# The order of the last group of a feed-forward in two token halves: the first half's out products ahead of the second half's gate

## The reference

```python
def swiglu(h, w_in, w_out):
    g, u = jnp.split(h @ w_in, 2, axis=-1)
    return (jax.nn.silu(g) * u) @ w_out
...
x = x + gt_f * rmsnorm(swiglu(h, w_ffn_in[l], w_ffn_out[l]), g_post_ffn[l])
...
def sandwich(x, fn, g_pre, g_post, shift, scale, gate, res_w):
    h = modulate_2(rmsnorm_2(x, g_pre), shift, scale)
    y = rmsnorm_2(fn(h), g_post)
    return x + res_w * gate[:, None, :] * y
```

## Time and profile before

| | |
|---|---|
| time, median of 3 runs | 2835.96 us (2835.62 to 2836.16) |
| time of the profiled execution | 2833.18 us |
| its span, first to last instruction | 2831.4 us |
| mean granted TensorE clock | 0.987 of full speed |
| PE busy | 2736.9 us, 97% |
| DVE, POOL, ACT busy | 1595.9, 1230.3, 1078.3 us |

### The profile page before, as it was taken

One profiled execution on the slowest core, in us unless ns is written; L12 is line 12 of the kernel. 1 busy time (PEld: TensorE's weight loads), 2 busy tenths in 40 slices (PEclk: granted clock), 3 DMA queues, 4 the chain that ended last, 5 costly groups with the idle time before them and its releaser, 6 DMA issues.

```text
span 2831.4 us, 41285 instructions
## 1 busy us (share of the span) xinstructions
PE 2736.9 (97%) x15742; PEld 2360.6 (83%) x15742; DVE 1595.9 (56%) x2593; ACT 1078.3 (38%) x1817; POOL 1230.3 (43%) x643
## 2 busy tenths in 40 slices
PE   8989999999999999899999999999999999999998
PEld 6778788888899799888888888888877788888887
DVE  6788565667777668655565555655553522422223
ACT  3267333223444457442222332222454833422222
POOL 0333444445555533344455344554433344444443
PEclk7999999999999999999999999999999999999999
DMA  5323555434576312424444334443323233133321
GB/s 236 97 57 94 193 198 189 149 134 135 178 241 228 107 37 60 142 92 161 148 156 156 120 134 149 156 170 134 107 66 105 82 97 97 58 107 96 96 89 60
DMA packets 103865, 361.70 MB, mean 128 GB/s; under 512 B 12449, under 2 KB 14625, under 8 KB 102305
## 3 DMA queue, kind: packets, MB, share of 16 engines
q1 hardware_dynamic: 103714, 359.63, 38.5%
HBM read 338.61 MB, written 2.10 MB: 120 GB/s over the span
## 4 chain that ended last, share of the span: by engine, by line
PE 85%; DVE 8%; ACT 2%; DMA 2%; issue 2%; POOL 1%; SPq 0%; ACTq 0%; DVEq 0%
PE ps L346 71%; PE ps L2264 3%; PE ps L2252 2%; PE ps L2234 2%; PE ps L760 1%; PE ps L570 1%; DVE negm L2313 1%; PE ps L422 1%; DVE dump L405 1%; DMA raw<-w_stream 1%; PE ps L2457 1%; PE ps L2026 1%; PE ps L2237 1%; ACT w_hi L317 1%; DVE h_lo L619 1%
## 5 line engine op out<-in xcount | busy, mean ns | idle before, releaser
L323 POOL TENSOR_TENSOR w_lo<-raw,w_hi 128x1024 fp32r<-128x1024 f32 x421 | 1069.8, 2549 | 1226.4 <-ACT w_hi L317 1193.6
L317 ACT ACTIVATE w_hi<-raw 128x1024 fp32r<-128x1024 f32 x441 | 460.3, 1056 | 1167.0 <-PE ps L346 1098.8
L346 PE MATMUL ps<-n_hi,w_hi 128*128 128x512 f32 (+1 forms) x1744 | 640.0, 367 | 10.5 <-DVE n_lo L867 9.5
L346 PE MATMUL ps<-n_lo,w_hi 128*128 128x512 f32 (+1 forms) x1744 | 628.1, 360 | 0.0
L346 PE MATMUL ps<-n_hi,w_lo 128*128 128x512 f32 (+1 forms) x1744 | 628.0, 360 | 0.0
L346 PEld LDWEIGHTS ps<-n_hi,w_hi 128*128 128x128 f32 x1744 | 329.7, 189 | 66.3 <-DVE n_lo L867 9.8
L346 PE MATMUL ps<-h_hi,w_hi 128*128 128x512 f32 (+1 forms) x1096 | 364.7, 348 | 8.8 <-DVE h_lo L619 3.8
L346 PEld LDWEIGHTS ps<-n_lo,w_hi 128*128 128x128 f32 x1744 | 329.9, 189 | 51.1 <-issue 1.9
L346 PEld LDWEIGHTS ps<-n_hi,w_lo 128*128 128x128 f32 x1744 | 329.6, 189 | 49.6
L346 PE MATMUL ps<-h_lo,w_hi 128*128 128x512 f32 (+1 forms) x1096 | 357.4, 341 | 0.0
L346 PE MATMUL ps<-h_hi,w_lo 128*128 128x512 f32 (+1 forms) x1096 | 357.1, 341 | 0.0
(11 more groups left out here) (325 smaller groups left out, 3806.2 us busy)
## 6 DMA issues: line engine op xcount, KB each, us to landing
raw<-w_stream SPq DMA_DIRECT2D x441, 512.0 KB, 3.7
modraw<-mod_stream SPq DMA_DIRECT2D x128, 512.0 KB, 3.8
mod_extra<-mod_stream SPq DMA_DIRECT2D x48, 512.0 KB, 4.8
mod_pair<-mod_first SPq DMA_DIRECT2D x7, 1024.0 KB, 12.5
l_qs<-l_q_hi SPq DMA_DIRECT2D x32, 128.0 KB, 2.3
l_qs<-l_q_lo SPq DMA_DIRECT2D x32, 128.0 KB, 2.3
l_qs<-l_q_hi SPq DMA_DIRECT2D x16, 192.0 KB, 2.9
l_qs<-l_q_lo SPq DMA_DIRECT2D x16, 192.0 KB, 3.5
```

Of the source, the lines that this page charges most:

```text
L317: nc.scalar.activation(w_hi[:, c % RING, :], raw[:, c % RING, :], ACT.Copy).then_inc(hi_ready, 1)
L323: nc.gpsimd.tensor_tensor(w_lo[:, c % RING, :], raw[:, c % RING, :], w_hi[:, c % RING, :].bitcast(F32), ALU.subtract).then_inc(lo_ready, 1)
L346: mm = nc.tensor.matmul(out, w[a], x[b][:, off:off + n], start=first and i == 0, stop=last and i == 2)
```

## The change

In the last group of the three feed-forwards the order becomes: gate and up of the first half, all out products of the first half, gate of the second half with the four post sums of the first half inside it, up of the second half with the spread of the first half inside it, out products of the second half. The out products of a half are now written as all eight products on the first hidden block, then a wait for the low part, then all eight on the second; before, only the four even ones went ahead of that wait. Pre sums of the first half stand after products 1, 4 and 7 of the second pass (before: 4, 6 and 7). The second half's up moves from PSUM bank 1 to bank 3, since bank 1 is now in use by `post_two`. ACT does the first half's squares and root before the second half's silu, with a second `root_ahead` after that silu and the split of block c + 4 behind it. DVE does total and inverse before `mult(1)` and places the first two `post_two` around `low(1)`. POOL does the three `post_added` before the split of d0.

```diff
-    HALF_GATE, HALF_UP, HALF_OUT, PRODUCTS = (3, 0), (1, 1), ((5, 6, 2, 7), (5, 6, 0, 7)), 1
+    HALF_GATE, HALF_UP, HALF_OUT, PRODUCTS = (3, 0), (1, 3), ((5, 6, 2, 7), (5, 6, 0, 7)), 1
...
-        def outs(e, between, beside):
-            for n in range(0, KC, 2):
-                out(e, n, [0])
-                if n == 6 and between:
-                    between()
-            pe.wait_ge(half_hid_lo, 2 * j + e + 1)
-            for n in range(KC):
-                mm = out(e, n, [1] if n % 2 == 0 else [0, 1])
-                if e == 1 and n == KC - 1:
-                    mm.then_inc(w_used, 2)
-                elif n % 2 == 1:
-                    mm.then_inc(half_out, 1)
-                if n in beside:
-                    beside[n]()
+        def outs(e, beside):
+            off, w = HALVES[e]
+            for b in range(2):
+                if b == 1:
+                    pe.wait_ge(half_hid_lo, 2 * j + e + 1)
+                for n in range(KC):
+                    mm = product(tiles(c + 2 + b)[n], (f["hi"][:, b, :], f["lo"][:, b, :]),
+                                 [(half(HALF_OUT[e][n // 2], n % 2), off, w)], (b, n % 2) == (0, 0), (b, n % 2) == (1, 1))
+                    if b == 1 and e == 1 and n == KC - 1:
+                        mm.then_inc(w_used, 2)
+                    elif b == 1 and n % 2 == 1:
+                        mm.then_inc(half_out, 1)
+                    if b == 1 and n in beside:
+                        beside[n]()
...
         pe.wait_ge(hid_ready, CREDIT + f["m"] + 2 * g + 1)
-        part_block(1, 0, HALF_GATE[1])
         pe.wait_ge(lo_ready, c + 4)
         pe.wait_ge(out_free, CREDIT + 8 * g)
-        outs(0, None, {5: post(0, 0), 7: post(0, 1)})
-        part_block(1, 1, HALF_UP[1], {1: post(0, 2), 3: post(0, 3)})
+        outs(0, {})
+        part_block(1, 0, HALF_GATE[1], {2: post(0, 0), 4: post(0, 1), 6: post(0, 2), 7: post(0, 3)})
+        pe.wait_ge(half_silu, 2 * j + 1)
+        part_block(1, 1, HALF_UP[1], {5: lambda: post_spread(pe, h, 0)})
...
-            outs(1, lambda: post_spread(pe, h, 0), {})
+            outs(1, {})
...
-        outs(1, lambda: post_spread(pe, h, 0), {4: pre(0), 6: pre(1), 7: pre(2)})
+        outs(1, {1: pre(0), 4: pre(1), 7: pre(2)})
...
         hidden_hi(0)
+        root_ahead()
+        for i in range(HPAIRS):
+            post_square(act, h, 0, i)
+        post_root(act, h, 0)
         silu(1)
         root_ahead()
         split_hi(act, c + RING)
-        for i in range(HPAIRS):
-            post_square(act, h, 0, i)
         hidden_hi(1)
-        post_root(act, h, 0)
...
+        post_total(dve, h, 0)
+        post_inverse(dve, h, 0)
         mult(1)
-        post_total(dve, h, 0)
+        post_two(dve, h, 0, 0, post_slot, PRODUCTS)
         low(1)
-        post_inverse(dve, h, 0)
+        post_two(dve, h, 0, 1, post_slot, PRODUCTS)
...
-            split_lo(pool, d0)
             for j in range(ADDED):
                 post_added(pool, h, 0, j)
+            split_lo(pool, d0)
```

More of the change, by code:

```diff
@@ L1124, in part_block @@
                     after[k]()
-        def out(e, n, bs):
+        def outs(e, beside):
             off, w = HALVES[e]
[L1128 to L1131, removed]
-        def outs(e, between, beside):
-            for n in range(0, KC, 2):
-                out(e, n, [0])
-                if n == 6 and between:
-                    between()
-            pe.wait_ge(half_hid_lo, 2 * j + e + 1)
-            for n in range(KC):
-                mm = out(e, n, [1] if n % 2 == 0 else [0, 1])
-                if e == 1 and n == KC - 1:
-                    mm.then_inc(w_used, 2)
-                elif n % 2 == 1:
-                    mm.then_inc(half_out, 1)
-                if n in beside:
-                    beside[n]()
+            for b in range(2):
[10 more added lines that the diff above has]
+                        beside[n]()
         def post(e, i):
@@ L1406, in last_halves_dve @@
             add(0, i)
+        post_total(dve, h, 0)
+        post_inverse(dve, h, 0)
         mult(1)
-        post_total(dve, h, 0)
+        post_two(dve, h, 0, 0, post_slot, PRODUCTS)
         low(1)
-        post_inverse(dve, h, 0)
+        post_two(dve, h, 0, 1, post_slot, PRODUCTS)
         if h == 4:
-            post_two(dve, h, 0, 0, post_slot, PRODUCTS)
-            post_two(dve, h, 0, 1, post_slot, PRODUCTS)
             for i in range(HPAIRS):
@@ L1422, in last_halves_dve @@
             return
-        for i in range(HPAIRS):
-            post_two(dve, h, 0, i, post_slot, PRODUCTS)
+        post_two(dve, h, 0, 2, post_slot, PRODUCTS)
+        post_two(dve, h, 0, 3, post_slot, PRODUCTS)
         add(1, 0)
```

## The result

The changed kernel takes 2841.23 us (median of 13 executions; 2836.62 to 2845.88) against 2835.96 us (13 as well; 2832.43 to 2837.67): ratio 1.0017, with a 95% interval of 1.0009 to 1.0025. Run a second time, it came to 1.0010 (1.0001 to 1.0019). So it is slower by about 0.1 to 0.2%. That is inside the forecast's bound of "no change"; the median lies on the upper edge of the forecast's range (2841.2).

What follows compares the result with a forecast made beforehand. TensorE, busy 97% of the span, was taken as the bound, so order matters only where PE stands still. 2 x 0.3 (order) + 2 x 1.3 (clock) - 0.75 (end) = +2.45 us on 2835.96: 2838.4, range 2834.6 to 2841.2.

Steps and rivals of the forecast that it cites:

- POOL's and ACT's queues: In h = 1 and 2, ACT's late split and POOL's two splits delay the first pre sum; PE idles about 3.2 us.
- The out block: First half's out products wait for POOL's low parts of both out blocks: a new PE stall of 0.46 us.
- The order without the clock: Last groups of h = 1 and 2: +0.3 us each before the clock is counted, bounds 0 and +1.0.
- The clock: After the idle in h = 1 and 2, 3.4 us at half clock cost 1.3 us each, bounds 0 and 1.5.
- Rival A: Clock stays at 1.00 after the pause in one or both stages: 2835.8, or 2837.1 with one fall; chance 0.27.
- The end: In h = 4, DVE's residual products after the adds start 0.75 us earlier: -0.75 us, bounds -0.3 and -1.2.
- nothing changes: In h = 4, from the residual products after the adds to the end, DVE sets the pace and no time changes.
- upper bounds: Order at most +1.0 and clock 1.5 us in each of h = 1 and 2; h = 4 at -0.3 us.
- Rival B: POOL is done sooner, pre sums are not late, DVE products set the gain: -4.95 us, 2831.0; chance 0.05.
- rival C: POOL is later still, with longer idle and half clock; with 1 us more, +7.85 us, 2843.8; chance 0.07.

Runs made afterwards that it cites:

- best version: Changed kernel with ACT's c + 4 split before the root, POOL's pre pairs before c + 5's split, second out block awaited only at use: 0.9968, 0.9972 of kernel before.
- idle filled: Changed kernel plus seven unread matmuls ahead of the first pre sum in h = 1 and 2: 0.9988 and 0.9993 of the kernel before.
- early split: Changed kernel with ACT's split of block c + 4 ahead of the root: 0.9985 of the kernel before, median 2833.12 us against 2836.70.
- later load: Changed kernel with ACT's second root_ahead (table load and root) behind both splits instead of ahead of them: 0.9994 of the kernel before.
- first pair ahead of c + 5: Changed kernel with POOL's first pre pair between its splits of c + 4 and c + 5: 1.0010 of the kernel before.

## Why the prediction was right

**POOL's and ACT's queues.** Every step from the root to the first pre sum came where the prediction had it, counted from the group's start: ACT's split 20.89 us in (predicted 20.77), POOL's splits 22.01 (21.89), the first pre sum 27.46 (27.4). Its idle was 3.23 (3.2). The kernels that move ACT's split or the load show that this path is the cause, and the later load that time taken off it goes whole out of PE's idle (1.49 us of each).

**The out block.** 0.35 us of idle, predicted 0.46 from issue to issue (6.26 from the gate to the first out product, less 5.76, gives 0.50 on that scale). The row names no releaser, but POOL's splits of the out blocks end at 1590.85, 0.10 us before that product starts, and without the wait for the second of them, in the best version, the idle is gone. In h = 4 of the best version, where only this wait differs, the group is 0.57 us shorter than with the new order alone (40.14 to 40.71).

**The order without the clock.** Predicted +0.3 a group, measured +0.2 (idle filled).

**The clock.** Predicted to fall in both groups, at 1.3 us each; it fell in all four groups of the two traces, and costs 1.51. The prediction took off 0.2 us for a part of the 3.4 us that could lie in the idle itself. None did: the fall came 0.3 to 1.3 us after PE had gone on, so all 3.4 us were paid. Rival A (no fall in one or both groups) did not happen in these two traces; what the other executions did is not known.

The Trainium skill ("TensorE: Matmul & The Clock Gate", section on HAM oscillation) has the group after such a wait begin at the low clock. The traces agree that the clock falls, but the work after the wait began at 1.00 and kept it for 0.3 to 1.3 us.

The drain of 1380 ns that the Trainium skill ("ScalarE: Activation LUTs", section on what ACT_TABLE_LOAD costs) adds to every switch is not seen: in the chain above 0.01 us lies between each load and the operation behind it and 0.02 us ahead of the second load, and moving that load together with its root took away 1.49 us of idle, not 2.5 or more.

**The end.** Predicted -0.75 us. With the clock at 0.50 at the last spread the old order takes 41.96 us and the new one 41.21: -0.75. With the fall behind the spread the new order takes 40.71, and the old one, with the fall near the spread's end, 41.49: -0.78. So the term was right, like against like; but "nothing changes" from the residual products on left out the spread, which is PE's and costs half a microsecond more or less by the clock, in either order. In the traces of the new order it ran at the low clock in five of nine (in a sixth for part of it), in neither of the best version, and in one of two of the old order; whether the order makes that likelier stays open.

With 0.2 and 1.5 us in each of the two groups and -0.75 at the end the sum is +2.65, where +2.45 was forecast. The largest error of size is in the clock, 0.2 us a group, and half of that is made up by the order, 0.1 us a group the other way. By the two traces as they fell the groups give 3.1 and 3.2 us. The medians differ by 5.3 us and, the second time, by 3.6; the intervals reach from 2.6 to 7.1 and from 0.3 to 5.4 us, and no run here tells whether what is over 3.2 us is more than the spread of the executions. The longer stretch between the groups of h = 1 and 2, 2.9 and 2.6 us in the two traces, would cover it. That the first median still lies on the edge of the range is partly luck: the forecast's own upper bounds add up to +4.7 us, 2840.7, and the range reached 0.5 us further without a term for it.

Rival B (pre sums not late) and rival C (idle of over 4 us) did not happen in the changed kernel. The best version shows a time like B's to be there once both queues are put right: B was given -4.95, it has -5.9, of which 0.57 in h = 4 come from the out block's wait, which B did not move.

## What to carry to other kernels

When work moves on one engine, write down for every other engine what now stands in front of its next urgent item. Here PE's order gained, and the split of a block that PE did not need for another 16 us had slid behind a root and two table loads in ACT's queue, and with its neighbour in front of an urgent pair in POOL's. Look for the engine's idle time before its waits, and put the work that is not urgent there: that turned +0.1% into -0.3%. And a wait on PE has two prices, the wait and the matmuls after it; a filler of unread matmuls separates the two in one run.

## What the runs showed of the hardware that was not expected

With two waits of 0.94 and 1.24 us, 3 us apart, came 10.2 us at granted clock 0.50 in one group and 3.4 us in the next, while single waits of 1.41 to 1.44 us (kernel before, early split) left it at 1.00 and those of 1.74 us (later load) did not. Cutting this wait in two didn't save the clock, then.

But the length of a wait alone doesn't decide. Some 8 to 10 us ahead of the groups of h = 1 and 2, in code that no run changes, PE waits for `y` in every trace, and the wait differs from one execution to the next. A fall came with 10 of these 26 waits. They lasted 2.00 to 3.16 us, and the 16 without a fall 1.25 to 2.99 us. The shortest with a fall (first pair ahead of c + 5) and the longest without one (idle filled), each with its granted clock behind it:

```profile
1569.73 0.79 PE L346 MATMUL ps<-ffn_hi,w_hi 128*128 128x512 f32 x1 [2.00 <-DVE y L1338]
1569.80:1573.10 3.30, 3.30 (x8) 2.62 (x9) 0.88 (x2) 0.00 (x0) 2.77 (x2) 0.50 0.46 161
```
```profile
1572.66 0.50 PE L346 MATMUL ps<-ffn_hi,w_hi 128*128 128x512 f32 x1 [2.99 <-DVE y L1342]
1572.70:1581.00 8.30, 8.30 (x37) 6.83 (x37) 3.94 (x6) 0.00 (x0) 2.85 (x2) 1.00 0.42 129
```

A fall of the clock matters even where PE does nearly nothing: four matmul records of 128x128 between two DVE operations took 1.22 us in place of 0.71, and that put half a microsecond on the kernel's end.
